# Expert items of 32 slots instead of 64, in a mixture-of-experts streaming encoder step

## The reference, cut to what matters

```python
# hier_moe: top-1 of 4 groups, then top-2 of the 8 experts in it
out = 0
for e in range(32):                       # w_gate, w_up: 1024 x 512; w_down: 512 x 1024
    hdn = silu(xn @ w_gate[e]) * (xn @ w_up[e])
    out = out + combine[:, e:e+1] * (hdn @ w_down[e])
x = x + out                               # then the final RMSNorm
```

## Time and profile before

| | us |
|---|---|
| median of 3 runs | 926.37 |
| lowest and highest | 925.6, 927.48 |
| the profiled execution, its own time | 926.79 |
| its span in the profile | 925.0 |
| PE busy in the span | 828.0 (90%) |
| DVE busy | 559.7 (61%) |
| ACT busy | 309.2 (33%) |

### The profile page before, as it was taken

The page is one execution under the profiler, slowest core; times in us unless marked ns, Lnnn a source line. Parts: engine busy times, 40 slices in busy tenths (PEclk is TensorE's granted clock), DMA queues, the critical chain, the costliest instruction groups (busy, mean ns, idle before and its releaser), DMA issues.

```text
span 925.0 us, 22551 instructions
## 1 busy us (share of the span) xinstructions
PE 828.0 (90%) x8411; PEld 625.0 (68%) x8412; DVE 559.7 (61%) x1516; ACT 309.2 (33%) x522; POOL 270.1 (29%) x136
## 2 busy tenths in 40 slices
PE   2999999979999999459699988887999999999993
PEld 2999999969999998436355555444656555555562
DVE  3056987899633241655377675556666666656766
ACT  4432875463347531831122211122121222221112
POOL 3745899776667884210000000000000000000000
PEclk9999999989999999769799999999999999999997
DMA  5734333343333322839799999999999999999801
GB/s 208 231 112 128 126 122 119 125 132 116 123 136 130 104 86 76 341 159 355 323 391 423 422 423 422 423 422 422 421 422 422 421 423 422 423 422 423 344 0 68
DMA packets 53128, 250.00 MB, mean 270 GB/s; under 512 B 6554, under 2 KB 6554, under 8 KB 28516
## 3 DMA queue, kind: packets, MB, share of 16 engines
q1 hardware_dynamic: 49184, 244.86, 66.9%
q10 hardware_dynamic: 3908, 4.67, 1.8%
HBM read 246.76 MB, written 2.75 MB: 270 GB/s over the span
## 4 chain that ended last, share of the span: by engine, by line
PE 71%; DMA 15%; DVE 6%; issue 3%; ACT 2%; POOL 1%; ACTq 0%; SPq 0%; DVEq 0%; POOLq 0%
PE bank L1303 27%; PE bank L1429 15%; DMA ring<-in_exp_w_up 14%; PE bank L1472 9%; PE bank L1391 7%; PE bank L1422 5%; PE bank L1301 4%; DVE bank L930 2%; PE bank L1461 2%; DMA stage<-in_norm_g 1%; POOL w_lo L496 1%; PE bank L1345 1%; ACT w_hi L616 1%; PE bank L1364 1%; PE bank L1266 1%
## 5 line engine op out<-in xcount | busy, mean ns | idle before, releaser
L496 POOL TENSOR_TENSOR w_lo<-raw,w_hi 128x2048 fp32r<-128x2048 f32 x40 | 184.6, 4618 | 80.6 <-ACT w_hi L616 80.5
L1429 PE MATMUL bank<-ring,cvb 128*32 128x256 f32 x2816 | 168.6, 393 | 42.1 <-DMA ring<-in_exp_w_up 21.0
L1429 PEld LDWEIGHTS bank<-ring,cvb 128*32 128x32 f32 x2816 | 93.3, 113 | 130.3 <-issue 83.6
L1303 PE MATMUL bank<-x_hi,w_hi 128*128 128x384 f32 x448 | 150.8, 337 | 0.2 <-DVE ua L949 0.2
L1303 PE MATMUL bank<-x_hi,w_lo 128*128 128x384 f32 x448 | 149.8, 334 | 0.0
L1303 PE MATMUL bank<-x_lo,w_hi 128*128 128x384 f32 x448 | 149.7, 334 | 0.0
L930 DVE SCALAR_TENSOR_TENSOR bank<-ub,vec,bank 128x256 f32<-128x256 f32 (+1 forms) x416 | 137.1, 411 | 0.0
L1472 PE MATMUL bank<-ring,cvb 128*64 128x512 f32 x560 | 127.9, 599 | 0.0
L1179 DVE SCALAR_TENSOR_TENSOR cvb<-bank,slot_coef,cvb 64x256 f32<-64x256 f32 x70 | 31.2, 487 | 128.0 <-ACT cvb L799 128.0
L616 ACT ACTIVATE w_hi<-raw 128x2048 fp32r<-128x2048 f32 x40 | 76.6, 1919 | 84.9 <-PE bank L1303 76.5
L808 ACT ACTIVATE y_hi<-bank 64x512 fp32r<-64x512 f32 x70 | 41.4, 591 | 175.8 <-PE bank L1472 174.9
(11 more groups left out here) (218 smaller groups left out, 1075.6 us busy)
## 6 DMA issues: line engine op xcount, KB each, us to landing
ring<-in_exp_w_gate SPq DMA_DIRECT2D x64, 1024.0 KB, 18.6
ring<-in_exp_w_up SPq DMA_DIRECT2D x64, 1024.0 KB, 20.6
ring<-in_exp_w_down SPq DMA_DIRECT2D x64, 1024.0 KB, 19.9
raw<-in_w_in SPq DMA_DIRECT2D x28, 1024.0 KB, 5.2
raw<-in_w_out_a SPq DMA_DIRECT2D x4, 1024.0 KB, 5.0
raw<-in_w_out_b SPq DMA_DIRECT2D x4, 1024.0 KB, 4.9
raw<-in_w_o SPq DMA_DIRECT2D x4, 1024.0 KB, 4.9
out<-n_tok ACTq DMA_DIRECT2D x3, 512.0 KB, 2.7
```

The lines of the kernel that those rows point to most:

```text
L496: pool.tensor_tensor(w_lo[u % NW][:, :, :], raw[u % NW][:, :, :], w_hi[u % NW][:, :, :].bitcast(F32), ALU.subtract).then_inc(lo_ready, 1)
L1303: ins = pe.matmul(b, wp[:, k % UK, cols], xp[:, k, :], start=start, stop=stop)
L1429: last = pe.matmul(gate_and_up(second)[q * TQ:(q + 1) * TQ, :], xe[:, k, second * TQ:(second + 1) * TQ], wide(slots[q // 2])[:, k, q % 2 * ...
```

## The change

T becomes 32. An item is up to 32 slots, always with four column tiles, in gate, up and in down (four quarters of 256 output columns). With the counts above this makes 44 items instead of 35. The two experts in each loop round stay, and so do the ring and SP's order; 44 - 16 = 28 items sum back, and one sum stands at the end. The second call of gate and up with its `If`, the table of quarters, its matmul and the clearing of a PSUM half go. `pick` is made by two wide operations, the coefficients by one wide operation, the four 32-row pieces of `y_hi` and `y_lo` by four operations each.

```diff
-    T = 64
-    TQ = T // 2
+    T = 32
+    TILES = P // T
+    SIDES = 2
...
-        Y = bank[3]
-
-        def gate_and_up(second):
-
-            return bank[1 + second][:, second * QE:(second + 1) * QE]
+        Y = bank[3][:, 0:D // TILES]
+        GU = bank[1][:, 0:QE]
...
@@ act
             def item(i, side, c):
                 act.wait_ge(gate_up_done, i + 1)
 
-                for second in range(2):
-                    act.activation(sig[:, second * QE:(second + 1) * QE], gate_and_up(second)[0:T, :], ACT.Silu)\
-                       .then_inc(sig_ready, 1)
+                act.activation(sig, GU[0:2 * T, :], ACT.Silu).then_inc(sig_ready, 1)
...
-                for h in range(2):
-                    act.activation(y_hi[side * T:(side + 1) * T, h * HALF:(h + 1) * HALF],
-                                   Y[h * T:(h + 1) * T, :], ACT.Copy).then_inc(y_hi_ready, 1)
+                for q in range(TILES):
+                    act.activation(y_hi[side * T:(side + 1) * T, q * QE:(q + 1) * QE],
+                                   Y[q * T:(q + 1) * T, :], ACT.Copy).then_inc(y_hi_ready, 1)
...
@@ dve
-            def pick_tokens(pick_base, pick_n):
-
-                for i in range(NT):
-                    dve.tensor_scalar(pick[:, i, :], iota[:, :], slot_rem[:, 0, i:i + 1], None, ALU.is_equal)\
-                       .then_inc(pick_half, 1)
-                for i in range(NT):
-                    dve.wait_ge(pick_half, pick_base + i + 1)
-                    last = dve.scalar_tensor_tensor(pick[:, i, :], iota[:, :], slot_rem[:, 1, i:i + 1],
-                                                    pick[:, i, :], ALU.is_equal, ALU.add)
-                last.then_inc(picked, 1)
+            def pick_tokens(pick_n):
+
+                dve.tensor_tensor(chosen, iota[:, :].unsqueeze(1).to_broadcast([P, 2 * NT, T]),
+                                  slot_rem.rearrange("p c i -> p (c i)").unsqueeze(2).to_broadcast([P, 2 * NT, T]),
+                                  ALU.is_equal).then_inc(chosen_ready, 1)
+                dve.wait_ge(chosen_ready, pick_n + 1)
+                dve.tensor_tensor(pick, chosen[:, 0:NT, :], chosen[:, NT:2 * NT, :], ALU.add).then_inc(picked, 1)
...
-            pick_tokens(0, 0)
-
-            link(dve.tensor_reduce(more, more_each, AX.X, ALU.add))
-            dve.tensor_scalar(quarters_b, ones[0:NE, :], more, 1.0, ALU.mult, ALU.add).then_inc(counts_ready, 1)
+            pick_tokens(0)
...
-            def next_coefficients(n):
-
-                for c in range(2):
-                    dve.scalar_tensor_tensor(at_slot[:, c, :], spread_rows[:, c, :], own_slot[:, 2:3],
-                                             spread_rows[:, 2 + c, :], ALU.is_equal, ALU.mult,
-                                             accum_out=coef_part[:, c:c + 1]).then_inc(coef_half, 1)
-                dve.wait_ge(coef_half, n * 2 + 2)
-                for second, found in enumerate((slice(T, P), slice(0, T))):
-                    dve.tensor_tensor(slot_coef[T:P, second:second + 1], coef_part[found, 0:1],
-                                      coef_part[found, 1:2], ALU.add).then_inc(slot_coef_ready, 1)
+            def next_coefficients():
+
+                flat = spread_rows.rearrange("p c n -> p (c n)")
+                dve.scalar_tensor_tensor(at_slot.rearrange("p c n -> p (c n)"), flat[:, 0:2 * N],
+                                         own_slot[:, SIDES:SIDES + 1], flat[:, 2 * N:4 * N], ALU.is_equal, ALU.mult,
+                                         accum_out=slot_coef[:, 0:1]).then_inc(slot_coef_ready, 1)
...
-                for h in range(2):
-                    dve.wait_ge(y_hi_ready, i * 2 + (h + 1))
-                    cols = slice(h * HALF, (h + 1) * HALF)
+                for q in range(TILES):
+                    dve.wait_ge(y_hi_ready, i * TILES + (q + 1))
+                    cols = slice(q * QE, (q + 1) * QE)
...
@@ pe
-                    with pe.If(second_slots):
-                        gate_up(part, slots, 1)
-                    gate_up(part, slots, 0).then_inc(done, 1)
+                    for k in range(part * KB // 2, (part + 1) * KB // 2):
+                        for q in range(TILES):
+                            last = pe.matmul(GU[q * T:(q + 1) * T, :], xe[:, k, :],
+                                             wide(slots[q // 2])[:, k, q % 2 * QE:(q % 2 + 1) * QE],
+                                             start=(k == 0), stop=(k == KB - 1))
+                    last.then_inc(done, 1)
...
-                for second in range(2):
-                    cols = hid[:, second * QE:(second + 1) * QE].rearrange("t (q c) -> t c q", c=HK // 2)
-                    for c2 in range(HK // 2):
-                        last = pe.transpose(turned[:, :, c2, second, :], cols[:, c2, :], ident[0:T, 0:T])
+                cols = hid.rearrange("t (q c) -> t c q", c=HK // 2)
+                for c2 in range(HK // 2):
+                    last = pe.transpose(turned[:, :, c2, :], cols[:, c2, :], ident[0:2 * T, 0:2 * T])
...
-                        for h in range(2):
-                            last = pe.matmul(Y[h * T:(h + 1) * T, :], hidT[:, k, :],
-                                             deep(slots[2])[:, k, h * HALF:(h + 1) * HALF],
+                        for q in range(TILES):
+                            last = pe.matmul(Y[q * T:(q + 1) * T, :], hidT[:, k, :],
+                                             deep(slots[2])[:, k, q * QE:(q + 1) * QE],
                                              start=(k == 0), stop=(k == HK - 1))
```

More of the change, by code:

```diff
@@ L806, in item @@
                 act.wait_ge(down_done, i + 1)
-                for h in range(2):
-                    act.activation(y_hi[side * T:(side + 1) * T, h * HALF:(h + 1) * HALF],
-                                   Y[h * T:(h + 1) * T, :], ACT.Copy).then_inc(y_hi_ready, 1)
[L811 to L816, removed]
+                for q in range(TILES):
+                    act.activation(y_hi[side * T:(side + 1) * T, q * QE:(q + 1) * QE],
+                                   Y[q * T:(q + 1) * T, :], ACT.Copy).then_inc(y_hi_ready, 1)
+            with act.Fori(0, NE // SIDES) as pair:
+                for side in range(SIDES):
+                    e = pair * SIDES + side
+                    n = act.value_load(table[0:1, bass.ds(e, 1)], min_val=1, max_val=N // T)
+                    first = act.value_load(table[0:1, bass.ds(e + NE, 1)], min_val=0, max_val=MAX_ITEMS - 1)
+                    back_first = act.value_load(table[0:1, bass.ds(e + (2 * NE + 1), 1)], min_val=0,
                                                 max_val=MAX_ITEMS - 1)
@@ L899, in _ @@
             dve.wait_ge(consts, 13)
-            dve.memset(own_slot[T:P, 0:1], -BIG).then_inc(own_slot_ready, 1)
-            dve.memset(own_slot[0:T, 1:2], -BIG).then_inc(own_slot_ready, 1)
-            odd = own_slot[T:P, 1:2]
-            dve.tensor_scalar(odd, odd, -float(T), None, ALU.add).then_inc(own_slot_ready, 1)
-            for g in range(P // TQ):
-                own = own_slot[g * TQ:(g + 1) * TQ, 2:3]
-                first_of = TQ if g < 2 else 0
-                dve.tensor_scalar(own, own, float(first_of - g * TQ), None, ALU.add).then_inc(own_slot_ready, 1)
+            dve.memset(own_slot[:], -BIG).then_inc(own_slot_ready, 1)
+            dve.wait_ge(own_slot_ready, 1)
+            for g in range(TILES):
+                rows = slice(g * T, (g + 1) * T)
+                for col in ((g, SIDES) if g < SIDES else (SIDES,)):
+                    dve.tensor_scalar(own_slot[rows, col:col + 1], lane[rows, :], -float(g * T), None, ALU.add)\
+                       .then_inc(own_slot_ready, 1)
             conv_b_at = {}
@@ L1075, in _ @@
             link(dve.tensor_scalar(more_each, steps[:], cnt, None, ALU.is_lt))
-            every_second = more_each[:, 1:N // TQ - 1].rearrange("e (n two) -> e n two", two=2)[:, :, 0]
-            link(dve.tensor_reduce(more, every_second, AX.X, ALU.add))
+            link(dve.tensor_reduce(more, more_each, AX.X, ALU.add))
             dve.tensor_scalar(ntile_b, ones[0:NE, :], more, 1.0, ALU.mult, ALU.add).then_inc(counts_ready, 1)
@@ L1381, in _ @@
             end_aux(pe.matmul(b[:, 0:2 * NE + 1], ntile_b, table_sums[:, :], start=True, stop=True))
-            pe.wait_ge(counts_ready, 2)
-            b = start_aux(aux("quarters"))
-            end_aux(pe.matmul(b[:, 0:NE], quarters_b, table_sums[:, 0:NE], start=True, stop=True))
             def gather(blocks):
@@ L1421, in combine, with item @@
                     for part, y in enumerate((y_hi, y_lo)):
-                        last = pe.matmul(b[:, :], back_to[:, t * P:(t + 1) * P], y[:, h * HALF:(h + 1) * HALF],
+                        last = pe.matmul(b[:, :], back_to[0:SIDES * T, t * P:(t + 1) * P], y[0:SIDES * T, h * HALF:(h + 1) * HALF],
                                          start=(part == 0), stop=(part == 1))
                 last.then_inc(combined, 1)
```

(10 more changed lines are left out.)

125 lines of the change are left out of this document (56 added, 69 removed).

## The result

The changed kernel takes **965.84 us** (median of 4 runs, 964.74 to 967.39) against 926.79 us (median of 4 runs beside it): ratio 1.0428, 95% interval 1.0415 to 1.0441. The forecast was 961.0 and slower. The profiled run's span is 963.0 us, 38.0 more than before.

What follows compares the result with a forecast made beforehand. Loads were taken to set the pace to about 655 us, mostly PE from expert 17 on. 11 us before expert 17 plus 23.7 after gave 34.7 on 926.8, 961.5, so 961 against the 926.4 median; range 942 to 984.

Steps and rivals of the forecast that it cites:

- Down, items, sums back: Per item, down takes 1.83 us instead of 3.58; 44 items; 28 sums back in the loop instead of 19.
- Before expert 17: Start to expert 17: experts 0 and 1 become two items each, slots come free 9.5 us later, +11 in effect.
- I take the stop, since nothing of the change removes a loop turn: First loop turn: the 7.1 us stop comes again; without it the load stream is only 5 us later.
- The cheap case: Whole kernel: no stop at the first turn and no DVE waits, 946 to 950 us; chance 0.12.
- 17 c items, 8 odd: From expert 17 on: c items (with a sum back) 10.65 us, odd ones 7.6; 181.1 + 60.8 = 241.9 us.
- VectorE's chain: DVE between two sums back takes 6.8 us against PE's 6.3; PE waits 12 x 0.5 = 6 us.
- waits for loads: From expert 17 on: heavy experts keep ring slots for three items, so PE waits for loads, 10 us.
- plus 0.15 each: Hand-over on PE added to each item; 3.8 us in all from expert 17 on.
- Loads at the pace all the way: Rival, whole kernel: gather cheaper, DVE chain below PE, loads set the pace; about 925 us; chance 0.05.
- Evictions in four pieces: Rival, DVE: each `y_lo` piece near 0.69 us, chain 8.0, 15 us more waits; 976 to 985 us; chance 0.12.
- Jumps back: Rival, inner loop from expert 17 on: four jumps cost the first turn's 7.1 us each; 987 us; chance 0.05.
- a down that does not pack: Rival, down: four tiles do not pack, 25 x 1.75 = 44 us more; 1005 us; chance 0.04.

Runs made afterwards that it cites:

- the longer down: Changed kernel with down in two column tiles of 512 columns again and y read out in two pieces; 978.41 us, a single run.
- the reads moved: Changed kernel with the odd expert's register reads inside the even expert's item: PE alone 967.53 us; PE and VectorE, coefficients behind `y_lo`, 962.99 us.
- the reads doubled: Three more register reads on PE per expert, six instead of three in the changed kernel: 1033.14 us; same addition in the kernel before: 1001.22 us.
- A loop of 2476 PE instructions: Changed kernel with four experts sharing one sum back, seven item bodies in the loop; 1061.86 us, and 959.94 us with two bodies (728 instructions).

## Why the prediction was right, and where its terms were off

The time fell inside the range, 4.8 us over the forecast. Two errors cancelled in part: 8 us too many were counted ahead of expert 17 and 10.6 too few behind it. So it is partly luck that the total came so near; the direction is not.

**Down, items, sums back**: right. 1.86 us for 1.83, 44 items, 29 sums. The packing was as the row of gate and up said.

**Before expert 17: +2.9 us, not +11.** Expert 17's gate and up end at 666.13, so in effect they start at 662.5 against 659.55. The step that failed is "I take the stop, since nothing of the change removes a loop turn": the first turn costs 1.92 us, not 7.1, and the first item's gate and up run at full clock (3.66). The clock from 440 to 460 us is 1.00 (0.74 before). Expert 4's first load is issued at 454.86, against 453.88 and 463 forecast. The cheap case's first half was the true one. Why the 7.1 us stand there before and not after was not tested.

**From expert 17 to the last sum back: 284.8 us, not 274** (662.5 to 947.26; before 250.5). Term by term:

| | forecast | measured |
|---|---|---|
| 17 c items, 8 odd | 181.1 + 60.8 = 241.9 | 17 x 11.05 + 8 x 7.92 = 251.2 |
| seven loop turns | 6 | 7 x 1.87 = 13.1 |
| hand-overs | 3.8 | 7 x 1.37 = 9.6 |
| jumps back inside an expert | 2 | in the next term |
| VectorE's chain | 6 | 4 x 0.65 = 2.6 |
| the end | 4.5 | 4.4 |
| waits for loads (measured: what is left over) | 10 | 3.9 |

Of the 3.9 us, 2.2 are a wait that the profile shows ahead of L1403 at 801.57 and about 1 is gate and up at a lower clock around it (3.85 for 3.66, 2.42 for 1.93). With 0.7 us more behind the last sum back, 2.9 + 34.3 + 0.7 is the 38.0 between the spans.

- **Items**: the gather of a c item takes 0.55 + 1.00 + 0.55 = 2.10 us, 29 ns a matmul where 25 were taken from the earlier trace rows; the sum back 3.16 instead of 3.05, transposes 0.38 for 0.31. The Trainium skill ("TensorE: Matmul & The Clock Gate", section on the back-to-back issue gap) has a floor of about 25 ns up to 64 columns; neither width comes down to it here: 30 to 34 ns at 64 columns, 27 to 31 at 32. Between those two the columns do count, but little.
- **Hand-overs and turns**: the step that failed is "plus 0.15 each" with 6 us for the turns, carried over from a row in which 3.58 us of down covered them. The cover was what the change took away, and the text gave it no name. 12.9 us, the largest miss. That these are the register reads is shown by the longer down (gap gone), by the reads moved (gap gone, item longer by 0.7 us, or 1.9 where the clock fell), and by the reads doubled (0.65 us each).
- **VectorE's chain**: 6.69 us from sum back to sum back against 6.8 forecast, right. But it decides at 4 places, not 12: an odd item after a c item finds `y_lo` ready, since the hand-over's 1.37 us lie ahead of it. Moving 1.1 us of it away gave 5 us.
- **Loads**: the dip (289 GB/s from 680 to 740 us) came as described, expert 17 to 20 holding their slots; the waits on the other side were shorter, since PE was slower too.

**The rivals.** Loads at the pace all the way: fell, PE's items averaged over 11 us. Evictions in four pieces: 418 ns each, six tenths of a whole one's 689; fell. Jumps back and a down that does not pack: fell.

**Why the change loses**, as far as the runs carry it: up to 655 us the loads hide what an item costs. Behind that the sum of items is 251.2 us for 238.5 before (+12.7: down is cheaper by 1.7 us an item, but there are seven more sums back of 3.16 and seven more gathers), turns and hand-overs are 22.7 us for some 7 (+16: reads that down no longer covers), and the rest, VectorE's chain at four places, the end and the loads, some 6.

## What to carry to other kernels

When a change shortens the last block of matmuls before a loop's branch, count the register reads behind it at their full length, 0.65 us a read here, and ask which block covers them now. Moving three of them in among short matmuls took away a stand of 1.4 us here and made the item 0.7 us longer, and where the clock then fell, in five places of eight, more than that was lost. A stand of two to four microseconds can cost twice, since the matmuls after it often, not always, run at a lower granted clock; so look at the clock behind each stand before a longer piece is put down to the work in it. And before making a stage's compute shorter, look at the rate of its loads in each stretch: at a flat 422 GB/s nothing is to be had there, only ahead of the stream and behind it.

## What was not expected of the hardware

- A loop of 2476 PE instructions was fetched anew all along (111 packets, stands of up to 15.0 us, 102 us in all), loops of 728 to 1368 were not (20 to 22 packets).
- A register read by PE costs 0.65 us when nothing covers it (three more: 1.9 us at a hand-over and at a turn). Three reads placed among matmuls of 25 to 60 ns each left 0.7 us in the item where they had stood 1.4 us outside it.
- Behind two such stands of 0.29 and 0.22 us the granted clock was 0.66 over 3.2 us. It was low in five items of eight, and 32 instructions of down took up to 3.64 us instead of 1.93.
- After a stand of 3.79 us the granted clock was 0.66 over the next 5 us, and 64 instructions of gate and up took 5.35 instead of 3.66 us; after 3.33 us, the next stand in the same run, they took 3.66.
- A branch on a register value ahead of down, with both forms behind it, left a stand of 0.23 us; with two register reads beside it the stand was 1.37 us.
